# A transformer kernel's feed-forward layers computed as 2x2 block products with seven multiplications

## What is computed

```python
def swiglu(xn, w_in, w_out):
    gate, up = jnp.split(jnp.einsum('btd,df->btf', xn, w_in), 2, axis=-1)
    return jnp.einsum('btf,fd->btd', jax.nn.silu(gate) * up, w_out)

for layer in range(DEPTH):
    xn = rmsnorm(x, norm_mix[layer])
    ...
    x = x + y
    x = x + swiglu(rmsnorm(x, norm_ffn[layer]), ffn_w_in[layer], ffn_w_out[layer])
```

## Time and profile before

| | |
|---|---|
| median of three runs | 1504.02 us |
| the profiled execution | 1506.59 us, its span 1504.9 us |
| mean granted TensorE clock | 0.970 |
| TensorE busy | 1433.1 us, 95% |
| VectorE, ScalarE, GpSimd busy | 544.2, 548.2, 591.9 us |
| feed-forward 0 | about 364 to 761 us |
| feed-forward 1 | about 1095 to 1492 us |

### The profile page before, as it was taken

The page is one execution under the profiler, slowest core; times in us unless marked ns, Lnnn a source line. Parts: engine busy times, 40 slices in busy tenths (PEclk is TensorE's granted clock), DMA queues, the critical chain, the costliest instruction groups (busy, mean ns, idle before and its releaser), DMA issues.

```text
span 1504.9 us, 27314 instructions
## 1 busy us (share of the span) xinstructions
PE 1433.1 (95%) x11099; PEld 1340.5 (89%) x11103; DVE 544.2 (36%) x1039; ACT 548.2 (36%) x879; POOL 591.9 (39%) x303
## 2 busy tenths in 40 slices
PE   4999899999999999999999988988999999999998
PEld 3778889899999999999988765947999999999997
DVE  5123536633421132123415975153343212321224
ACT  4423546534332243222355244143353323421222
POOL 1331222223544344434445356364334434443442
PEclk7998889999999999999999999899999999999999
DMA  4221111232323223322233320200222322232221
GB/s 142 80 75 43 46 53 54 78 93 65 110 84 107 71 85 87 109 69 75 81 97 82 71 88 2 71 8 15 85 84 85 111 84 70 84 112 70 81 74 59
DMA packets 208774, 114.34 MB, mean 76 GB/s; under 512 B 16692, under 2 KB 202936, under 8 KB 208696
## 3 DMA queue, kind: packets, MB, share of 16 engines
q1 hardware_dynamic: 203448, 109.50, 25.4%
q10 hardware_dynamic: 5248, 3.73, 0.8%
HBM read 107.26 MB, written 5.96 MB: 75 GB/s over the span
## 4 chain that ended last, share of the span: by engine, by line
PE 63%; issue 24%; POOL 9%; DVE 3%; ACT 1%; POOLq 0%; DVEq 0%; ACTq 0%
PE ps L983 55%; POOL w_lo L535 6%; PE ps L1078 4%; POOL arena L519 2%; PE ps L1306 1%; PE ps L1346 1%; PE ps L1318 1%; DVE small L1819 1%; POOL m_only L519 0%; DVE arena L1768 0%; PE ps L1337 0%; DVE arena L1787 0%; DVE arena L1804 0%; PE ps L1449 0%; ACT arena L847 0%
## 5 line engine op out<-in xcount | busy, mean ns | idle before, releaser
L535 POOL TENSOR_TENSOR w_lo<-w_raw,w_hi 128x1024 fp32r<-128x1024 f32 x202 | 499.8, 2478 | 830.4 <-ACT w_hi L598 830.4
L983 PE MATMUL ps<-x_hi,w_hi 128*128 128x272 f32 (+1 forms) x1952 | 412.0, 293 | 10.3 <-DVE arena L1628 6.1
L983 PE MATMUL ps<-x_hi,w_lo 128*128 128x272 f32 (+1 forms) x1952 | 408.6, 291 | 0.0
L983 PE MATMUL ps<-x_lo,w_hi 128*128 128x272 f32 (+1 forms) x1952 | 407.3, 291 | 0.0
L983 PEld LDWEIGHTS ps<-x_hi,w_hi 128*128 128x128 f32 (+1 forms) x1952 | 310.8, 191 | 17.4 <-issue 12.1
L983 PEld LDWEIGHTS ps<-x_lo,w_hi 128*128 128x128 f32 (+1 forms) x1952 | 310.8, 191 | 0.5
L983 PEld LDWEIGHTS ps<-x_hi,w_lo 128*128 128x128 f32 (+1 forms) x1952 | 308.5, 191 | 0.5
L598 ACT ACTIVATE w_hi<-w_raw 128x1024 fp32r<-128x1024 f32 x202 | 211.3, 1051 | 192.1 <-PE ps L983 142.9
L983 PE MATMUL ps<-o_hi,w_hi 128*128 128x272 f32 x960 | 199.6, 289 | 2.0 <-DVE arena L1687 1.1
L983 PE MATMUL ps<-o_hi,w_lo 128*128 128x272 f32 x960 | 199.2, 289 | 0.0
L983 PE MATMUL ps<-o_lo,w_hi 128*128 128x272 f32 x960 | 198.4, 288 | 0.0
(11 more groups left out here) (241 smaller groups left out, 1364.4 us busy)
## 6 DMA issues: line engine op xcount, KB each, us to landing
w_raw<-in_ffn_w_in SPq DMA_DIRECT2D x88, 512.0 KB, 3.8
w_raw<-in_ffn_w_out SPq DMA_DIRECT2D x32, 512.0 KB, 3.7
w_raw<-in_ab_w_in SPq DMA_DIRECT2D x28, 512.0 KB, 3.8
w_raw<-in_cd_w_in SPq DMA_DIRECT2D x13, 512.0 KB, 3.7
w_raw<-in_ffn_w_out SPq DMA_DIRECT2D x16, 384.0 KB, 3.3
w_raw<-in_ab_w_out SPq DMA_DIRECT2D x8, 512.0 KB, 4.1
arena<-in_x_prompt SPq DMA_DIRECT2D x4, 512.0 KB, 5.3
w_raw<-in_cd_w_in SPq DMA_DIRECT2D x8, 256.0 KB, 3.5
```

Of the source, the lines that this page charges most:

```text
L535: pool.tensor_tensor(wl[:, s, :], raw[:, s, :], wh[:, s, :].bitcast(F32), ALU.subtract).then_inc(lo_done, 1)
L983: mm = pe.matmul(ps[0:M, b + h, 0:HALF], w[:, s, k * M:(k + 1) * M], xs[x][:, k, h * HALF:(h + 1) * HALF], start=(begin and k == ks[0] and ...
```

## The change

Each two output tiles form a pair: gate and up of one hidden tile ("g", 22 a layer), or two output tiles of the down projection ("w", 4 for each part; the parts are now 4, 6, 6 and 6 hidden tiles, so 16 a layer). A pair is a 2x2 block product: weight blocks A11, A12 (first tile, first and second half of the k-blocks), A21, A22 (second tile); activation blocks B11, B12, B21, B22 (half of the k-blocks by half of the tokens). Seven products of half the k-blocks and half the tokens replace the eight:

S1 = A21+A22, S2 = S1-A11, S3 = A11-A21, S4 = A12-S2; T1 = B12-B11, T3 = B22-B12, T2 = T3+B11, T4 = B21-T2; P1 = A11 B11, P2 = A12 B21, P3 = S4 B22, P4 = A22 T4, P5 = S1 T1, P6 = S2 T2, P7 = S3 T3.

P1 and P6, P5 and P3 go on in one PSUM bank ("x"), P7 and P4 in another ("y"), P2 in a third ("z"); the intermediate states are copied out by ScalarE (p1b, u2b, u4b) for g pairs and added to x by VectorE for w pairs. Each product is made in the three passes. Its weight factor, raw or a sum, has its own high part (ScalarE, `factor_hi`) and low part (GpSimd, `ffn`), in slots of half the size, eight in a ring; VectorE forms the S (`weight_sum`). The T of x are formed in `add_back`/`split_x` by VectorE, those of the hidden blocks in `combine`, the low parts in `hidden_lo` (one instruction for an early tile of a part, two for a late one). The products of neighbouring pairs interleave: P6, P7, P5 of a pair, P1 of the next, P3, P2 of the next, P4. The down pairs of a part come after the first g pair of the next. All loops of the feed-forward are written out (no hardware loops). The eight cache loads and GpSimd's constants for layer 1 move behind the last g pair's products and behind feed-forward 0.

```diff
-    PART = 8
+    PARTS = [(0, 4), (4, 6), (10, 6), (16, 6)]
...
+    pairs = []
+    for r, (r0, n) in enumerate(PARTS):
+        hid = [("g", r, t + e * (n // 2)) for t in range(n // 2) for e in range(2)]
+        pairs += hid if r == 0 else hid[:1] + [("w", r - 1, m) for m in range(0, KT, 2)] + hid[1:]
+    pairs += [("w", len(PARTS) - 1, m) for m in range(0, KT, 2)]
+    NPAIR = len(pairs)
+    g_pairs = [p for p in range(NPAIR) if pairs[p][0] == "g"]
+    LAST_G = g_pairs[-1]
+    prods = [(0, "P1"), (0, "P2")]
+    for p in range(NPAIR):
+        more = p + 1 < NPAIR
+        prods += [(p, "P6"), (p, "P7"), (p, "P5")] + [(p + 1, "P1")] * more + [(p, "P3")]
+        prods += [(p, "P4")] + [(p + 1, "P2")] * more if p == LAST_G else [(p + 1, "P2")] * more + [(p, "P4")]
+    NPROD = len(prods)
+    at_prod = {key: n for n, key in enumerate(prods)}
+    FACTORS = {"P1": ("A11", "B11"), "P2": ("A12", "B21"), "P3": ("S4", "B22"), "P4": ("A22", "T4"),
+               "P5": ("S1", "T1"), "P6": ("S2", "T2"), "P7": ("S3", "T3")}
...
+        def bank(l, p, which):
+            if which == "z":
+                return ps[:, 4 + p % 2, 0:HALF]
+            return ps[:, (XB[l] if which == "x" else 2 - XB[l]) + p % 2, 0:HALF]
...
+            for c in range(C_F[0], C_F[0] + 2 * LAST_G + 6):
+                load(c)
             sp.wait_ge(m0_out, 16 * N_M0_OUT)
+            sp.wait_ge(prod_done, at_prod[LAST_G, "P4"] + 1)
...
+            for c in range(C_F[0] + 2 * LAST_G + 6, C_END):
                 load(c)
...
+            def ffn(l):
+                for n, (p, pr) in enumerate(prods):
+                    pool.wait_ge(u_hi, l * NPROD + n + 1)
+                    pool.tensor_tensor(half_slot(wl, l, n), factor(l, p, FACTORS[pr][0]), half_slot(wh, l, n).bitcast(F32),
+                                       ALU.subtract).then_inc(u_lo, 1)
...
+            def m1_constants():
+                pool.wait_ge(prod_done, NPROD)
...
+            def factor_hi(l, n):
+                p, a = prods[n][0], FACTORS[prods[n][1]][0]
+                if n >= 8:
+                    act.wait_ge(prod_done, l * NPROD + n - 7)
+                else:
+                    wait_done(act, C_F[l] - SLOTS + n // 2)
+                if a[0] == "S":
+                    act.wait_ge(s_added, 4 * (l * NPAIR + p) + int(a[1]))
+                else:
+                    c = C_F[l] + 2 * p + int(a[1]) - 1
+                    act.wait_ge(raw_landed[c % SLOTS], landed[c])
+                act.activation(half_slot(wh, l, n), factor(l, p, a), ACT.Copy).then_inc(u_hi, 1)
             def first_norm():
...
+                        hi(C_M1 + int(NPROD - n == 2))
+                    gated = pairs[p][0] == "g"
+                    gi = g_pairs.index(p) if gated else 0
+                    if gated and pr == "P1":
+                        act.wait_ge(prod_done, l * NPROD + n + 1)
+                        if gi >= 1:
+                            act.wait_ge(z_taken, b + g_pairs[gi - 1] + 1)
+                        act.activation(p1b, bank(l, p, "x"), ACT.Copy).then_inc(p1_taken, 1)
...
+                    if pr in ("P7", "P3") and p - 1 > LAST_G:
+                        final_x(2 * l + 2, pairs[p - 1][2] + int(pr == "P3"))
+                    if gated and pr == "P4":
+                        act.wait_ge(g_scaled, FT * l + gi + 1)
+                        act.wait_ge(x_taken, b + p + 1)
+                        act.activation(fsig, fg, ACT.Sigmoid).then_inc(f_sig, 1)
...
+            def product(l, n):
+                p, pr = prods[n]
...
+                b, kh, x = l * NPAIR, halves(p), FACTORS[pr][1]
+                pe.wait_ge(u_lo, l * NPROD + n + 1)
+                if pr == "P1":
+                    if p >= 2:
+                        pe.wait_ge(x_taken, b + p - 1)
+                    else:
+                        wait_freed(pe, C_F[l] - 2)
+                elif pr == "P2":
+                    if p >= 2:
+                        pe.wait_ge(z_taken, b + p - 1)
+                elif pr == "P6":
+                    pe.wait_ge(p1_taken, b + p + 1)
+                elif pr == "P5":
+                    pe.wait_ge(u2_taken, b + p + 1)
+                elif pr == "P3":
+                    pe.wait_ge(u4_taken, b + p + 1)
+                elif pr == "P7":
+                    if p >= 2:
+                        pe.wait_ge(y_taken, b + p - 1)
+                    else:
+                        wait_freed(pe, C_F[l] - 1)
+                elif pr == "P4":
...
+                first = (p == 0 if kind == "g" else i == 0) and pr in ("P1", "P2", "P6")
+                for k in range(kh):
+                    if first and kind == "g":
+                        pe.wait_ge(s_nl, DONE_X[1 + 2 * l] + (k + 1 if pr == "P1" else 4 + 2 * k + (1 if pr == "P2" else 2)))
+                    elif first:
+                        pe.wait_ge(h_lo, 3 * (11 * l + HID0[r] + k) + {"P1": 1, "P2": 2, "P6": 3}[pr])
+                    for a, (w, e) in enumerate(((0, 0), (0, 1), (1, 0))):
+                        mm = pe.matmul(out, wts[w][:, k * P:(k + 1) * P], xs[e][:, q + k, :],
+                                       start=(pr in ("P1", "P2", "P7") and k == 0 and a == 0), stop=(pr in ("P2", "P3", "P4") and k == kh - 1 and a == 2),
+                                       skip_group_check=True)
+                mm.then_inc(prod_done, 1)
...
+            def weight_sum(l, p, which):
...
+                s1, s2, s3, s4 = (factor(l, p, a) for a in ("S1", "S2", "S3", "S4"))
...
+                    before = at_prod[p - 1, ("P5", "P6", "P7", "P3")[which - 1]] + 1 if p > 0 else 0
+                    dve.wait_ge(u_lo, l * NPROD + before)
+                if which == 1:
+                    for e in range(2):
+                        dve.wait_ge(raw_landed[(c + e) % SLOTS], landed[c + e])
+                    dve.tensor_tensor(s1, a21, a22, ALU.add).then_inc(s_added, 1)
+                elif which == 2:
+                    dve.wait_ge(s_added, b + 1)
+                    dve.tensor_tensor(s2, s1, a11, ALU.subtract).then_inc(s_added, 1)
+                elif which == 3:
+                    dve.tensor_tensor(s3, a11, a21, ALU.subtract).then_inc(s_added, 1)
+                else:
+                    dve.wait_ge(s_added, b + 2)
+                    dve.tensor_tensor(s4, a12, s2, ALU.subtract).then_inc(s_added, 1)
...
+                def silu(p):
+                    h = FT * l + g_pairs.index(p)
+                    kind, r, t = pairs[p]
...
+                    dve.wait_ge(f_sig, h + 1)
+                    dve.tensor_tensor(fg, fg, fsig, ALU.mult).then_inc(f_mul, 1)
+                    dve.wait_ge(f_mul, 2 * h + 1)
+                    dve.tensor_tensor(fg, fg, rstd, ALU.mult).then_inc(f_mul, 1)
+                    dve.wait_ge(f_mul, 2 * h + 2)
+                    dve.wait_ge(y_taken, b + p + 1)
+                    dve.wait_ge(h_lo, 3 * (11 * l + HID0[r] + t % kh) + int(late))
+                    out = hf[:, 2:4, :] if late else hf[:, 0:8:7, :]
+                    dve.tensor_tensor(out, two(fg), two(fu), ALU.mult).then_inc(f_h, 1)
...
+                for p in range(NPAIR + 1):
+                    kind = lambda q: pairs[q][0] if 0 <= q < NPAIR else None
+                    was, now, then = kind(p - 1), kind(p), kind(p + 1)
+                    if was:
+                        ended(p - 1, "P4")
+                    if was == "g":
+                        dve.wait_ge(u2_taken, b + p)
+                        dve.wait_ge(f_h, FT * l + g_pairs.index(p - 1))
+                        dve.tensor_tensor(fu[:, first], u2b[g_pairs.index(p - 1) % 2], bank(l, p - 1, "y"), ALU.add).then_inc(y_taken, 1)
+                    elif was == "w":
+                        dve.wait_ge(u2_taken, b + p)
+                        add_to_x(p - 1, 1, first, "y").then_inc(y_taken, 1)
+                    early = was == "g" and p >= LAST_G
+                    if early:
+                        silu(p - 1)
+                        combine(p - 1)
+                        hidden_lo(p - 1)
+                    if p == LAST_G + 1:
+                        add_p2(p)
+                    if then:
+                        weight_sum(l, p + 1, 1)
+                    if now == "w":
+                        ended(p, "P6")
+                        add_to_x(p, 1, first, "x").then_inc(u2_taken, 1)
+                    if was == "g" and not early:
+                        silu(p - 1)
+                    if then:
+                        weight_sum(l, p + 1, 2)
+                    if now == "g":
+                        ended(p, "P2")
+                        dve.wait_ge(p1_taken, b + p + 1)
+                        dve.wait_ge(f_h, FT * l + g_pairs.index(p))
+                        dve.tensor_tensor(fg[:, first], p1b, bank(l, p, "z"), ALU.add).then_inc(z_taken, 1)
+                        dve.wait_ge(z_taken, b + p + 1)
                         dve.wait_ge(s_rs, 2 * l + 2)
```

(36 more changed lines are left out.)

524 lines of the change are left out of this document (327 added, 197 removed).

## The result

The changed kernel takes 1676.73 us (median of 4 runs, 1669.73 to 1681.42), the kernel before on the same chips 1506.55 (4 runs, 1503.4 to 1509.53): ratio 1.1126, 95% interval 1.1069 to 1.1183. The forecast was 1652.

What follows compares the result with a forecast made beforehand. TensorE's issue was taken to bound the feed-forward layers. Span 1504.9 + 142 (the two layers, with contention at the port) + 6 (edges) = 1653, as a median 1652 us; range 1550 to 1740.

Steps and rivals of the forecast that it cites:

- Bound and saving: Feed-forward layers, bound by TensorE's issue: seven products for eight, 2772 matmuls for 3168 a layer; two layers lose 99 us.
- The port: Gate pairs: GpSimd's subtractions and VectorE's two-SBUF instructions never run at once; together they want 13.9 us, above TensorE's 10.5.
- Gate pair: VectorE's pass of 9.5 us plus 4.9 and 1.0 for GpSimd's turns: 15.4 us, bounds 13.9 and 17.
- Rival 1: Gate pairs: the port is packed nearly without loss, 13.9 to 14.5 us a pair, total 1553 to 1590; chance 0.17.
- Down pairs: Down projection: 8.1 us a pair with 6 tiles, 6.0 with 4, against TensorE's 7.9 and 5.3.
- The last four pairs: End of a layer, with the next norm's split and squares: four port instructions each, +2 us a pair, 8 a layer.
- The edge: Start of a layer: longer chain from the last tile of x, 0 to 5 us a layer, 3 taken, +6 in all.
- 2 (faster): Gate pairs: short operations slip past each other, TensorE's pace returns, 10.5 us in place of 15.4, total 1415; chance 0.06.
- 3 (waits chain up): Gate pairs: VectorE's pass is held by a landing or ScalarE's order; over 17 us, total 1760 and more; chance 0.09.
- 4: Feed-forward: TensorE's clock falls because it stops between products; at half clock all through, 2100 us; chance 0.03.
- 5: Whole change: it does something else than seven products, matmul count other than 10,307; inside the 0.02 for no change.
- The signs: Right: gate pairs 14 to 17 us, TensorE idle in each; wrong: gate pairs at 10.5, or feed-forward clock under 0.95.

Runs made afterwards that it cites:

- E1: The changed kernel with GpSimd writing zeros for about as long, reading nothing, in place of the feed-forward weight factors' low parts: 1479.66 us.
- E2: The changed kernel with GpSimd's low parts of the feed-forward's weight factors left out except for the first 16 columns: 1476.54 us.
- E8: The changed kernel with 36 more matmuls into an unused bank where TensorE waits longest, at the changes from gate to down pairs: 1671.27 us.
- E9: The changed kernel with GpSimd forming the low parts of the feed-forward's weight factors for the first half of the columns only: 1510.78 us.
- E3: The changed kernel; in pairs 4 to 32 of each layer, one operand of VectorE's four weight sums is zeros read from PSUM: 1593.84 us.
- E6: The changed kernel; in pairs 4 to 32 of each layer, VectorE's four weight sums are cut to 16 columns each, both operands in SBUF: 1608.34 us.

## Why the prediction was right, and where its sizes were off

**Bound and saving.** 5544 matmuls in the two layers, 2 x 2772, as counted; the product of 12 takes 1.50 us wherever nothing holds it (the 10.59 of E1's gate pairs is 7 x 1.51). Right. Without contention 1480 was to be had (E1), not 1506.5 - 99 = 1407: E1's layers take 385 and 383 us where the matmuls take 347. Of 6.6%, 1.8% is left once starts and changes are paid.

**The port.** The step on which the forecast rests, right in kind and nearly in size. Holds of 1.15 and 0.58 add up to the measured turns of 1.74 and 1.70. Gate pair: 15.4 forecast; the 21 after the first have 14.84 on the mean (layer 0), 0.56 less. How many of the five subtractions at full price fall under VectorE's PSUM instructions after all was not counted. Rival 1 (packed, 13.9 to 14.5) is nearer to 14.84 than the forecast, and the handover does cost nearly nothing, as it said. It fell by the sum alone, and its sum had the down pairs at TensorE's pace and no tail. So the total doesn't decide between it and the forecast.

**What the mean hides.** The pairs are not alike: 10.6 for the first after a down block, where VectorE and GpSimd have got ahead, then 12.6 and 17.4 by turns, 20.3 for the last. In the last pair before a change the extra is the wait for the hidden blocks' low parts (64.1 us in 10 waits, the changes' own), in the others above all P4's wait for VectorE's sum (L1880, 56.3 us in 28): late hidden tiles bring five port instructions (three combinations, two low parts) where early ones bring two. The sum held it, as the mean of early and late, but as no step of its own.

**Down pairs.** 8.1 forecast, 8.7 on the mean of eight; 6.0 against 7.2 with four tiles. The steady ones have 7.9 to 8.1 and 5.6; the forecast left out that the first and the last of a block of four are next to a change (9.3 to 9.8 with six tiles, 7.9 and 8.6 to 9.8 with four). 5 + 5 us a layer.

**The last four pairs: the term most under-sized.** 40.4 forecast, 53.7 in layer 0, 46.4 in layer 1. The larger part is the first of the four: 16.3 and 17.7 us where the sum had 8.1 + 2. In the other parts a gate pair stands between the last hidden tile and the down pairs; here none does, and TensorE waits for the chain from silu to the low parts (kernel after, in order of time):

```profile
800.25 0.72 DVE L1791 TENSOR_TENSOR arena<-arena,rstd 128x544 f32<-128x544 f32 x1
...
803.26 1.01 DVE L1823 TENSOR_TENSOR o_lo<-arena,o_hi 128x816 fp32r<-128x816 f32 x1
...
804.33 0.60 PE L1244 MATMUL ps<-o_hi,w_hi 128*128 128x272 f32 x1 [5.32 <-DVE o_lo L1823]
804.34 1.43 POOL L624 TENSOR_TENSOR w_lo<-arena,w_hi 128x384 fp32r<-128x384 f32 x1 [4.71 <-ACT w_hi L702]
```

This is not the port: GpSimd stands for 4.7 us, VectorE's steps take their 0.72, and without the contention the same pair takes 15.3 (E1) and 15.5 us (E2, still with a wait of 4.6), while the waits of 6.0 to 7.9 us at the three earlier changes fall to 1.9 and less (layer 0). The forecast had no term for this wait. The second place is the last pair of layer 0, 17.1 us (10.1 in layer 1). The four more port instructions were priced at +2 a pair from 512-column turns; in the rows of that pair they meet the two low halves of 1024 columns for the next mixer:

```profile
836.17 5.64 POOL L617 TENSOR_TENSOR w_lo<-w_raw,w_hi 128x1024 fp32r<-128x1024 f32 x2
...
836.72 2.89 DVE L1837 SCALAR_TENSOR_TENSOR x_lo<-xT,par,x_hi 128x544 fp32r<-128x544 f32 x1
...
839.54 2.85 DVE L1668 TENSOR_TENSOR arena<-arena 128x544 f32<-128x544 f32 x1
...
843.24 0.57 PE L1244 MATMUL ps<-o_hi,w_hi 128*128 128x272 f32 x1 [5.26 <-DVE xT L1780]
```

Each turn costs 2.26 there instead of 1.15: the 2.9 us of the earlier trace rows stood in the rows and were not used for this place. Layer 1 has no next mixer. (Layer 0 turns the caches in this pair as well; how the 7 us divide was not tried.)

**The edge.** 3 us a layer forecast, 9 to 10 measured in layer 0 (7.0 of waits in the first pair and some 2.5 of half clock): TensorE stood 5.5 us for the first products' x, and came back at half clock:

```profile
371.45 0.60 PE L1244 MATMUL ps<-x_hi,w_hi 128*128 128x272 f32 x1 [5.55 <-DVE x_lo L1723]
371.84 0.43 PE L1244 MATMUL ps<-x_lo,w_hi 128*128 128x272 f32 x1
```

From 371.45 to 377.8 a matmul has 0.227 us in place of 0.1253, at 1.2 GHz; with the 24 recorded there some 2.5 us were lost. The upper bound of 5 us took the chain of the last tile of x alone. VectorE is at the last two tiles one after the other, and at the four sums ahead of them (start, us):
```profile
357.04 1.78 DVE L1747 TENSOR_TENSOR arena<-w_raw 128x512 f32<-128x512 f32 x1
...
361.64 0.71 DVE L1704 TENSOR_TENSOR xT<-ps,xT 128x544 f32<-128x544 f32 x1
...
367.08 0.72 DVE L1704 TENSOR_TENSOR xT<-ps,xT 128x544 f32<-128x544 f32 x1
...
370.68 0.72 DVE L1723 TENSOR_TENSOR x_lo<-arena,x_hi 128x544 fp32r<-128x544 f32 x1
```

The sums take 4.6 us, a tile 5.4, and TensorE waits for the 370.68 one. The cache loads and the constants cost nothing that can be seen, as said.

**The rivals.** 2 (faster) fell; and E1 shows that its price was too good as well (1480, not 1415). 3 (waits chain up) holds for single pairs, not for the mean. 4 is there in part (153 us of half clock in the two layers). 5 fell by the count.

**The signs.** Most of those named for "right" came: two-SBUF instructions at 1.4 to 1.6 us, PSUM ones at 0.43, the mean gate pair at 14.8. But single gate pairs lie between 10.6 and 20.3, the first after a down block runs at TensorE's pace, and TensorE waits for VectorE rather than for GpSimd's low half. And one sign named for "wrong" came too: a granted clock under 0.95 in the feed-forward (0.93 from 505 to 635 us). It didn't overturn the mechanism, since E1 and E2 give the loss back by taking only GpSimd's reading away, and the clock of the feed-forward rises with it (0.98 in E1). As a sign against the port it was badly chosen: TensorE's stops bring it about here, whatever causes them (E8 raised the clock by filling the longest).

In sum, against the layers' 969.1 us, the forecast had 27 too few: 19 too few in the last four pairs, 19 in the other down pairs, and 11 too many in the gate pairs with the edge. That the total came within 25 us is in part luck: the 11 cancel part of the 38.

## What to carry to other kernels

Count the requests: every VectorE instruction with two SBUF operands costs one whole subtraction of GpSimd while GpSimd has work queued, however short it is, and the loss is about what both together need beyond the bounding engine (worked out from the holds, borne out by E9's pair times). So putting one operand in PSUM (83 us in E3) gives more than trimming nearly all columns (68 in E6); merging short instructions should help by the same reasoning, but wasn't tried. Work taken from the bounding engine and given to two engines that share a port is worth only what both need together, not what each needs alone. And a scheme that saves an eighth of the matmuls must be priced at its changes and ends: here these alone took what the down projection saved. Look for the place where nothing stands between a result and its first use.
